# The attention's value tiles by way of device memory: one change to a hybrid encoder step

## The reference, cut

```python
aq, ak, av, mq, mk, mv, mi, mf, mo = split_in(rms_norm(x, norm1_g) @ w_in)
aq, ak = rms_norm(aq, q_norm_g), rms_norm(ak, k_norm_g)      # per head and half of 128
p = softmax(q @ k.T * scale + bias, masked by chunk)          # two score maps a head
o = (p[:, 0] - lam * p[:, 1]) @ v                             # v: the new av rows, for streams after 256 cached rows
att = rms_norm(o, subln_g) * (1 - lam_init)
hm = mlstm(mq, mk, mv, mi, mf, state)                         # matrix memory, gated by mo
x = x + concat(att, hm) @ w_out
y = x + square(relu(rms_norm(x, norm2_g) @ w_up)) @ w_down
```

## Time and profile before

| | |
|---|---|
| median of 3 runs (lowest, highest) | 1737.78 us (1736.31, 1738.28) |
| the profiled execution, its span | 1736.11 us, 1734.3 us |
| TensorE busy, granted clock | 1726.7 us, 1.00 |
| VectorE, ScalarE, GpSimd busy | 903.3, 654.3, 381.1 us |
| DMA | 291.83 MB, mean 168 GB/s |

### The profile page before, as it was taken

One profiled execution on the slowest core, in us unless ns is written; L12 is line 12 of the kernel. 1 busy time (PEld: TensorE's weight loads), 2 busy tenths in 40 slices (PEclk: granted clock), 3 DMA queues, 4 the chain that ended last, 5 costly groups with the idle time before them and its releaser, 6 DMA issues.

```text
span 1734.3 us, 24676 instructions
## 1 busy us (share of the span) xinstructions
PE 1726.7 (100%) x8472; PEld 1469.8 (85%) x8472; DVE 903.3 (52%) x1681; ACT 654.3 (38%) x1224; POOL 381.1 (22%) x544
## 2 busy tenths in 40 slices
PE   9999999999999999999999999999999999999999
PEld 8999999999987788888888888888888888888887
DVE  5634776555687655645433554343455334456333
ACT  5323754444354444333333333332333323333332
POOL 3321010002451251434000343000334100234100
PEclk9999999999999999999999999999999999999999
DMA  7685469999788585665444565334556444555542
GB/s 191 175 193 145 129 156 231 206 199 224 222 254 260 147 209 172 171 184 166 125 129 122 168 178 180 130 122 131 161 164 183 140 131 123 161 167 171 172 143 97
DMA packets 294446, 291.83 MB, mean 168 GB/s; under 512 B 96717, under 2 KB 201485, under 8 KB 294349
## 3 DMA queue, kind: packets, MB, share of 16 engines
q1 hardware_dynamic: 254886, 222.09, 46.3%
q0 software_dynamic: 24400, 64.58, 13.9%
q10 hardware_dynamic: 15062, 3.86, 1.1%
HBM read 259.84 MB, written 36.40 MB: 171 GB/s over the span
## 4 chain that ended last, share of the span: by engine, by line
PE 97%; DVE 2%; issue 0%; ACT 0%; DMA 0%; ACTq 0%; DVEq 0%
PE bank L685 9%; PE bank L686 9%; PE bank L639 9%; PE bank L640 9%; PE bank L638 9%; PE bank L684 9%; PE acc L539 8%; PE acc L540 8%; PE acc L541 8%; PE bank L2038 3%; PE ssb L684 2%; PE ssb L638 2%; PE ssb L685 2%; PE ssb L639 2%; PE ssb L686 2%; PE ssb L640 2%
## 5 line engine op out<-in xcount | busy, mean ns | idle before, releaser
L519 DVE TENSOR_TENSOR w_lo<-raw,w_hi 128x512 fp32r<-128x512 f32 x768 | 537.8, 706 | 760.8 <-ACT w_hi L510 760.1
L510 ACT ACTIVATE w_hi<-raw 128x512 fp32r<-128x512 f32 x768 | 482.7, 631 | 964.6 <-PE acc L541 197.3
L539 PE MATMUL acc<-a_hi,w_hi 128*128 128x400 f32 (+1 forms) x768 | 268.1, 349 | 0.2 <-DVE w_lo L519 0.2
L540 PE MATMUL acc<-a_lo,w_hi 128*128 128x400 f32 (+1 forms) x768 | 262.9, 342 | 0.0
L541 PE MATMUL acc<-a_hi,w_lo 128*128 128x400 f32 (+1 forms) x768 | 262.4, 342 | 0.0
L685 PE MATMUL bank<-w_lo,a_hi 128*128 128x512 f32 x640 | 253.1, 395 | 0.0
L686 PE MATMUL bank<-w_hi,a_lo 128*128 128x512 f32 x640 | 252.7, 395 | 0.0
L639 PE MATMUL bank<-w_lo,x2g_hi 128*128 128x512 f32 x640 | 252.4, 394 | 0.0
L640 PE MATMUL bank<-w_hi,x2g_lo 128*128 128x512 f32 x640 | 252.2, 394 | 0.0
L638 PE MATMUL bank<-w_hi,x2g_hi 128*128 128x512 f32 x640 | 252.1, 394 | 0.0
L684 PE MATMUL bank<-w_hi,a_hi 128*128 128x512 f32 x640 | 252.1, 394 | 0.0
(11 more groups left out here) (356 smaller groups left out, 1803.2 us busy)
## 6 DMA issues: line engine op xcount, KB each, us to landing
raw<-in_w_up SPq DMA_DIRECT2D x128, 512.0 KB, 3.8
raw<-in_w_down SPq DMA_DIRECT2D x128, 512.0 KB, 3.8
raw<-in_w_in SPq DMA_DIRECT2D x94, 512.0 KB, 4.7
raw<-in_w_out SPq DMA_DIRECT2D x32, 512.0 KB, 5.4
u_turned<-m POOLq DMA_DIRECT2D x192, 64.0 KB, 3.1
stage<-u_turned POOLq DMA_DIRECT2D x16, 768.0 KB, 6.0
vc<-in_cache_v POOLq DMA_DIRECT2D x32, 256.0 KB, 6.4
kc<-in_cache_k SPq DMA_DIRECT2D x128, 64.0 KB, 3.3
```

The lines of the kernel that those rows point to most:

```text
L510: e.activation(w_hi[:, q], raw[:, slot, 4 * (q % 2):4 * (q % 2) + 4, :], ACT.Copy).then_inc(hi_ready, 1)
L519: e.tensor_tensor(w_lo[:, q], raw[:, slot, 4 * (q % 2):4 * (q % 2) + 4, :], w_hi[:, q].bitcast(F32), ALU.subtract).then_inc(lo_ready, 1)
L539: e.matmul(out, w_hi[:, q, kk], hi[:, k, at], start=k == 0, stop=False, skip_group_check=True)
L540: e.matmul(out, w_hi[:, q, kk], lo[:, k, at], start=False, stop=False, skip_group_check=True)
```

## The change

The value tiles are no longer turned by TensorE. SP stores each, as it is, to a new tensor `av_d` in device memory (`av_out`): the store of value n stands in SP's queue behind the weight load of tile 19 + n, and waits for the tile and for the store before it. GpSimd loads two values at a time (`av_back`), in 13 DMAs of 128-byte pieces, so that 32x32 blocks of rows by columns lie on the right partitions, into `vc[:, 1]`, once both are stored; these loads stand behind the block copies 10, 12, 14 and 15. VectorE turns two values with two block transposes (`turn_av`), at the second quarter of tiles 21 and 23 and at slots 3 and 7 of the attention's plan, where the step is listed ahead of the key turns of its slot. The cached values of stream 1, which use the same `vc[:, 1]`, are loaded after the last turn. Two constants' semaphores are merged into others on the way.

```diff
-AV_AHEAD = T_M - T_AV - 2
+AV_TURNS = {(5, 1): 0, (7, 1): 1}
...
-    plan += [(4 * (j - AV_AHEAD), "av", j) for j in range(AV_AHEAD, 8)] + [(4 * j + 1, "ko", j) for j in range(8)]
+    plan += [(3, "av", 2), (7, "av", 3)] + [(4 * j + 1, "ko", j) for j in range(8)]
...
+        av_d = nc.dram_tensor("av_d", [8, P, TOK], F32).ap()
...
+            av_blk = vc[:, 1].rearrange("p x (r i t) -> p x r i t", i=8, t=32)
...
-            for b in range(2):
-                load_values(b)
+            load_values(0)
+            e.memset(av_blk[0:32, :, 3, :, TAIL:32], 0.0).then_inc(S("wt_padded"), 1)
...
+            def av_back(n):
+
+                e.wait_ge(S("av_out"), 16 * 2 * (n + 1))
+                if n >= 2:
+                    e.wait_ge(S("av_turned"), n - 1)
+                else:
+                    e.wait_ge(S("wt_padded"), 2)
+                at = 2 * n * P * TOK
+                for j in range(4):
+                    rows = slice(32 * j, 32 * j + 32)
+                    for r in range(3):
+                        dma(av_blk[rows, n % 2, r], bass.AP(tensor=av_d.tensor, offset=at + STARTS[r] + 32 * j,
+                                                            ap=[[TOK, 32], [32 * TOK, 8], [1, 32]]), f"av_in{n % 2}")
+                dma(av_blk[0:32, n % 2, 3, :, 0:TAIL], bass.AP(tensor=av_d.tensor, offset=at + STARTS[3],
+                                                               ap=[[TOK, 32], [32 * TOK, 8], [1, TAIL]]), f"av_in{n % 2}")
+
             for n in range(16):
                 e.wait_ge(acc_free, 9 + n)
...
+                if n in (10, 12, 14, 15):
+                    av_back((n - 9) // 2)
+
-            read_out(e, *[("av", j) for j in range(8)])
+            e.wait_ge(S("av_turned"), 4)
+            load_values(1)
...
-            with e.Fori(1, T_M // 2) as p:
+            with e.Fori(1, T_AV // 2 + 1) as p:
...
+            def av_out(n):
+
+                if 0 <= n < 8:
+                    e.wait_ge(acc_free, T_AV + n + 1)
+                    if n:
+                        e.wait_ge(S("av_out"), 16 * n)
+                    e.dma_start(av_d[n], m1[:, n]).then_inc(S("av_out"), 16)
...
+            for t in range(T_AV + 2, T_M):
+                load_tile(e, t // 2, t % 2, w_in[0], 0, P * t)
+                av_out(t - 3 - T_AV)
...
                 load_tile(e, t // 2, t % 2, w_in[0], 0, col, behind=behind_load(t))
+                av_out(t - 3 - T_AV)
                 spill(t - 3)
...
-                if q == 0 and u >= 2:
-                    take_av(u - 2)
+                if (u, q) in AV_TURNS:
+                    turn_av(AV_TURNS[u, q])
...
-            def take_av(n):
-
-                b = take(e, ("av", n))
-                cs = slice(n * P, (n + 1) * P)
-                e.tensor_copy(av_rows[:, 0:3, cs], b[:, 0:3 * P].rearrange("p (r n) -> p r n", n=P))
-                taken(e.tensor_copy(av_rows[0:TAIL, 3, cs], b[0:TAIL, 3 * P:4 * P]), ("av", n))
+            def turn_av(n):
+
+                cs = slice(n * DV, (n + 1) * DV)
+                e.wait_ge(S(f"av_in{n % 2}"), 16 * 13 * (n // 2 + 1))
+                e.transpose(av_rows[0:32, 3, cs], av_blk[0:32, n % 2, 3].rearrange("p i t -> p (i t)"))
+                e.transpose(av_rows[:, 0:3, cs],
+                            av_blk[:, n % 2, 0:3].rearrange("p r i t -> p r (i t)")).then_inc(S("av_turned"), 1)
...
-                if q == 0 and u >= 2:
-                    turn_av(u - 2)
-                elif q == 1:
+                if q == 1:
...
-            def turn_av(n):
-                e.wait_ge(acc_free, T_AV + n + 1)
-                turn_rows(("av", n), m1[:, n])
...
-                    if what == "av":
-                        turn_av(n)
-                    elif what == "first_scores":
+                    if what == "first_scores":
```

More of the change, by code:

```diff
@@ L242, in plan_banks @@
     for t in range(T_AV, T_M):
-        if t >= T_AV + 2:
-            u.add(("av", t - T_AV - 2), (2, 4)[t % 2])
         for x in range(2):
@@ L247, in plan_banks @@
     for _, what, n in ATT_PLAN:
-        if what == "av":
-            u.add(("av", n), (2, 4)[n % 2])
-        elif what == "first_scores":
+        if what == "first_scores":
             u.add(("s", STEPS[n], 0), 0)
@@ L728, in _ @@
             dma(xn[0:TAIL, 3, later], x_prompt[0, 2 * P - META:SEQ, later], "x_small")
-            e.memset(gw[:].bitcast(F32), 0.0).then_inc(S("gw_padded"), 1)
+            e.memset(gw[:].bitcast(F32), 0.0).then_inc(S("consts"), 1)
             e.tensor_copy(ones_r[:], ones[:]).then_inc(S("consts"), 1)
@@ L1071, in rows_and_gates @@
                     e.wait_ge(S("gw_in"), 16)
-                    e.wait_ge(S("gw_padded"), 1)
+                    e.wait_ge(S("consts"), 4)
                     e.activation(gw_hi, gw_raw[:], ACT.Copy).then_inc(S("gw_hi_made"), 1)
@@ L1167, in att_work @@
                         if n == 0:
-                            e.wait_ge(S("wt_padded"), 2)
+                            e.wait_ge(S("wt_padded"), 3)
                         if is_pair(step):
@@ L1530, in _ @@
             e.tensor_copy(n_t[:, 0:PAST].rearrange("p (x r) -> p x r", r=32),
-                          bias_s[:, 0:PAST].rearrange("p (r x) -> p x r", x=8)).then_inc(S("bias_ordered"), 1)
-            e.wait_ge(S("bias_ordered"), 1)
+                          bias_s[:, 0:PAST].rearrange("p (r x) -> p x r", x=8)).then_inc(S("bias_masked"), 1)
+            e.wait_ge(S("bias_masked"), 2)
             e.tensor_copy(bias_s[:, 0:PAST], n_t[:, 0:PAST]).then_inc(S("bias_masked"), 1)
@@ L1646, in att_work @@
                     if what == "av":
-                        take_av(n)
+                        turn_av(n)
                     elif what == "ko":
@@ L1659, in att_work @@
                         e.wait_ge(S("w_new_zero"), 2)
-                        e.wait_ge(S("bias_masked"), 2)
+                        e.wait_ge(S("bias_masked"), 3)
                         e.wait_ge(S("lam_ready"), 1)
@@ L2124, in qk_sums @@
                 u = t - T_AV
-                if q == 0 and u >= 2:
-                    turn_av(u - 2)
-                elif q == 1:
+                if q == 1:
                     if u == 0:
-                        e.wait_ge(S("consts"), 4)
+                        e.wait_ge(S("consts"), 5)
                     e.wait_ge(S("n_low"), u + 1)
```

## The result

The changed kernel takes 1743.3 us (median of 6 runs, 1742.8 to 1744.6), the kernel before beside it 1736.3 us (6 runs, the three of the table before among them): ratio 1.004, 95% interval 1.003 to 1.005. So it is 7.0 us slower. The forecast was 1746.7 us, 8.9 us more than the 1737.78 us of the three runs, with 1738 to 1753 us as its range.

A forecast was written before the change was run, and what follows sets the result against it. TensorE, busy for the whole span, was taken as the bound. Earlier start -3.3, later key turn +10.9 and slow restart +1.3 gave +8.9 us on 1737.78: 1746.7 us, range 1738 to 1753 us.

The forecast's parts named there:

- The turns are gone: On TensorE, eight value turns of four transposes leave, 0.44 us each, 3.5 us in all; six before the chain's start, 2.6 us.
- VectorE and the other stores are neutral: VectorE swaps 5.3 us of copies for 5.4 us of block transposes; the sync queue's eight stores hold nothing up.
- The store of value 7 stands behind 16 key loads: In the sync queue, tile 23's store waits behind two groups of eight key loads, until 255.52 us in the old clock.
- The store's landing: The last value store to device memory lands after 6.0 us (2.5 to 10.7), the median of the 200 KB spills.
- The last piece: On GpSimd, the last of 13 loads begins 6.96 us after the first and lands after 4.8 us (2.3 to 9.2).
- the 10 us that the prediction named as a sign: On VectorE, the last value turn comes 10 us after its slot if the forecast is right.
- The slow restart: TensorE's first matmuls after about 12 us idle run at half pace, costing 1.3 us (bounds 0 and 1.3).
- The sum: Whole kernel: -3.3 for the earlier start, +10.9 for the later key turn, +1.3 for the restart, +8.9 us.
- second wait: A sign on TensorE: a further wait at the pair's 'out' or for weight splits would mean the burst delays weights.
- more late: Rival: value stores and stream 1's cache burst at 275 us, delaying a weight load some 5 us; 1752 us, chance 0.08.
- In time: Rival: values 6 and 7 arrive before the key turn, gaining 3.5 us of turns and 0.3 of wait; 1734.0 us, chance 0.08.

The follow-up runs named there:

- run 1: Changed kernel with the store of value 7 issued between the two groups of key loads; 1740.3 us, ratio 1.0022 to the kernel before.
- run 6: Changed kernel with value 7's store between the key load groups and the last turn listed behind its slot's key turn; 1737.9 us, ratio 1.0007.
- run 2: Changed kernel with the last value turn at slot 11 instead of 7; 1740.8 us, ratio 1.0020 to the kernel before.
- run 7: Changed kernel with the last turn at slot 11 and without the three stores of the new values; 1733.8 us, ratio 0.9982.
- run 10: Changed kernel with the last turn at slot 11 and the stores of the new values issued later; 1735.3 us, ratio 0.9992.

## Why the prediction was right

- **The turns are gone and are worth 0.44 us each.** From the scaling of tile 16 to that of tile 23 VectorE's rows go from 180.17 and 249.31 us to 179.71 and 246.15: 69.14 against 66.44 us, six turns, 2.70 us (2.6 predicted). The rows, two before and two after:

```profile
180.17 0.57 DVE L1413 TENSOR_TENSOR m<-acc,rstd_x 128x400 f32<-128x400 f32 x1
...
249.31 0.57 DVE L1413 TENSOR_TENSOR m<-acc,rstd_x 128x400 f32<-128x400 f32 x1
```

```profile
179.71 0.57 DVE L1442 TENSOR_TENSOR m<-acc,rstd_x 128x400 f32<-128x400 f32 x1
...
246.15 0.57 DVE L1442 TENSOR_TENSOR m<-acc,rstd_x 128x400 f32<-128x400 f32 x1
```

- **VectorE and the other stores are neutral.** 903.2 us against 903.3. The turns of values 0 to 5 wait for nothing.
- **The store of value 7 stands behind 16 key loads.** As said: 252.87 us, against 255.52 less the 3.3 of the earlier start, 252.2.
- **The store's landing was mis-sized.** I took 6.0 us, the median of the spills, because the DMA engines are full here; it was 2.5, the low end. This is 3.5 us, the largest miss of a term. Those spills are of a later stage. The kernel before has rows of this one that I passed over: its three stores of the new values, on GpSimd's queue at 256.90 us, land after 6.6 to 8.4 us, and the sixteen key loads of the earlier trace rows, on the store's own queue, after 2.3 to 4.5, 3.3 in the median. The rows of the same queue and stage were the nearer ones. In runs 1 and 6, some 5 us earlier, the store takes 4.5 and 4.4 us.
- **The last piece** landed after 4.2 us (4.8 predicted), the turn took 1.2 us, and the key turn came right behind it. The first scores came 4.2 us later than before instead of 7.6, and TensorE waited 8.5 us instead of about 12. VectorE stood 6.3 us at the turn, not the 10 us that the prediction named as a sign.
- **The slow restart was mis-sized, too:** 2.44 us where I took 1.3, the most that the earlier trace rows gave: they have three matmuls at half pace, here it was the whole pass of the scores and ten more matmuls. So 1.3 us was no upper bound.
- **The sum:** 8.9 - 3.5 (store) - 0.6 (last piece) + 0.7 (the store's place) + 1.1 (restart) + 0.1 (the rest) = 6.7 us, and the runs have 7.0. That the sum is off by only 2 us is in part luck: two terms too large and two too small make up for each other. The forecast time is off by 3.4 us, and 1.5 of these are its base: the median of three runs, 1737.78 us, was 1736.32 with six.
- **No second wait.** The rival *more late* did not come. That the wait itself gave the DMA engines the time, as said against it, fits runs 2, 7 and 10 but wasn't tried by itself. Its burst of stores does harm as soon as the wait is taken away: 4.2 us in run 2, where it is a key load that is late, not a weight load. I had it as something that adds to the wait, and it stands in the wait's place.
- **In time** did not come either. Its price was 3.8 us less than the kernel before, and with the turn out of the way at slot 11 runs 2 and 7 show that this also needs the stores elsewhere: 4.1 us more with them, 2.8 us less without. The key loads ahead of the store held the queue for 7.53 and 5.78 us, which is what spoke against this rival.
  The Trainium skill (DMA: Bandwidth & Descriptors, Issuing engines are not separate DMA queues) calls the time to start a DMA usually small against the DMA's own. Load by load this trace agrees: these sixteen take 0.67 us each to issue and 3.9 us to land, in the median. The prediction set the page's sentence against the sum of sixteen issues, which the page doesn't speak of.

## What to carry to other kernels

When work goes from the busiest engine to a path over device memory, price the last piece first: what stands ahead of its store in the queue that issues it, and what stands behind the waiting instruction on the engine that takes it back. Then look at the stage where the moved transfers end up: where the DMA engines were full, as here, taking the first wait away gave a second one, and with the last turn at slot 11 the loss went only when other bytes were moved out of that stage. Price a long wait of TensorE at its length and a slow restart on top: here 2.4 us after 8.5.

## What the runs showed that I had not expected

- After 8.5 us without work TensorE ran at a granted clock of 0.50 for the first 5.4 us (268.86 to 274.30); the same wait filled with unused products left it at 1.00, and the whole was 2.1 us faster by the medians (1743.3 to 1741.2), 1.7 by the spans, with more work in it.
- The same store of 200 KB lands after 1.9 us in the median of the eight, after 2.5 us where it was issued at 252.87 us (DMA share 1.10 from 252 to 256 us) and after 4.5 us at 247.60 us in run 1 (1.03 and 1.20 in the two stretches of 4 us from 246 us on); the share hardly tells the two apart.
- The time to issue isn't fixed: the same store took 0.34 us to issue at 237.27 us (DMA share 0.52 from 236 to 239 us), 0.64 us behind the sixteen key loads (1.30 from 252 to 254 us), and between the two groups of them 1.18 us in run 1 and 0.73 in run 6. One key load of 64 KB took 6.5 us to issue in run 2, at 278.71 us, beside GpSimd's 2.6 MB.
